# Two unused margins in SBUF: other start addresses for the operands of a two-block kernel

## The reference

```
h   = modulate(rms_norm(x, g), shift, scale)            # first block
p   = h @ w_in                                          # 2048 x 3904
x   = x + gate * (rms_norm(concat(att, conv)) @ w_out)  # 2048 x 2048
u   = dwconv3(hf @ w_up)                                # 2048 x 11008
x   = x + gate * ((a * silu(g)) @ w_down)               # 5504 x 2048
z   = rms_norm(x) @ w_in_2                              # second block, 2048 x 10248
m   = sigmoid(g_a) * (A @ w_proj_a) + sigmoid(g_b) * (B @ w_proj_b)
x   = x + m @ w_out_2
x   = x + square(relu(rms_norm(x) @ w_up_2)) @ w_down_2 # 2048 x 8192 x 2048
out = rms_norm(x)
```

## Time and profile before

| | |
|---|---|
| median of 3 runs | 2872.16 us (2868.47 to 2873.35) |
| profiled execution, its own time | 2872.42 us |
| its span | 2870.6 us |
| TensorE busy | 2684.6 us (94%), weight loads 2571.9 us (90%) |
| VectorE, ScalarE busy | 1794.6 us (63%), 1224.7 us (43%) |
| granted TensorE clock, mean | 0.959 |
| DMA | 552.93 MB, mean 193 GB/s |

### The profile page before, as it was taken

One profiled execution on the slowest core, in us unless ns is written; L12 is line 12 of the kernel. 1 busy time (PEld: TensorE's weight loads), 2 busy tenths in 40 slices (PEclk: granted clock), 3 DMA queues, 4 the chain that ended last, 5 costly groups with the idle time before them and its releaser, 6 DMA issues.

```text
span 2870.6 us, 52211 instructions
## 1 busy us (share of the span) xinstructions
PE 2684.6 (94%) x21408; PEld 2571.9 (90%) x21408; DVE 1794.6 (63%) x2056; ACT 1224.7 (43%) x1407; POOL 20.8 (1%) x24
## 2 busy tenths in 40 slices
PE   4959977768899999999999999999999999999998
PEld 3659975348899999999999999999999999999998
DVE  3988965678766776576556455555555555555554
ACT  2733331223455554354454344444444443434433
POOL 0000000000000000000000000000000000000000
PEclk9989987769999999999999899999999999999999
DMA  4958953427566656656556455566556666666562
GB/s 156 384 195 315 331 171 120 147 88 282 188 191 201 195 182 204 192 163 220 183 171 186 130 173 166 161 188 199 196 178 184 191 197 192 190 196 193 196 206 103
DMA packets 288834, 552.93 MB, mean 193 GB/s; under 512 B 19434, under 2 KB 28632, under 8 KB 288024
## 3 DMA queue, kind: packets, MB, share of 16 engines
q1 hardware_dynamic: 287416, 548.10, 59.2%
q10 hardware_dynamic: 1248, 2.42, 0.3%
HBM read 548.35 MB, written 2.10 MB: 192 GB/s over the span
## 4 chain that ended last, share of the span: by engine, by line
PE 86%; DVE 9%; issue 2%; ACT 2%; DMA 1%; ACTq 1%; DVEq 0%; SPq 0%
PE half L1627 25%; PE half L1629 25%; PE half L1628 25%; DVE wlo L909 2%; PE half L1683 1%; DVE acc L931 1%; PE half L1661 1%; PE half L1663 1%; DVE acc L928 1%; PE half L1662 1%; DVE tmp L1233 1%; DMA raw<-in_w_ada 1%; PE half L1832 1%; PE half L1821 1%; PE half L1822 1%
## 5 line engine op out<-in xcount | busy, mean ns | idle before, releaser
L909 DVE TENSOR_TENSOR wlo<-raw,whi 128x1024 fp32r<-128x1024 f32 (+2 forms) x917 | 1096.7, 1209 | 815.8 <-ACT whi L511 813.6
L511 ACT ACTIVATE whi<-raw 128x1024 fp32r<-128x1024 f32 (+2 forms) x917 | 952.5, 1048 | 1195.0 <-PE half L1629 1033.6
L1627 PE MATMUL half<-hf,whi 128*128 128x256 f32 x2400 | 663.9, 277 | 6.2 <-DVE hf L986 5.1
L1628 PE MATMUL half<-hf,whi 128*128 128x256 f32 x2400 | 663.4, 276 | 0.0
L1629 PE MATMUL half<-hf,wlo 128*128 128x256 f32 x2400 | 663.4, 276 | 0.0
L1627 PE MATMUL half<-hid,whi 128*128 128x256 f32 x1712 | 474.0, 277 | 0.0
L1628 PE MATMUL half<-hid,whi 128*128 128x256 f32 x1712 | 473.4, 276 | 0.0
L1629 PE MATMUL half<-hid,wlo 128*128 128x256 f32 x1712 | 473.4, 276 | 0.0
L1627 PEld LDWEIGHTS half<-hf,whi 128*128 128x128 f32 x2400 | 451.4, 188 | 7.0 <-issue 5.5
L1629 PEld LDWEIGHTS half<-hf,wlo 128*128 128x128 f32 x2400 | 451.3, 188 | 0.0
L1628 PEld LDWEIGHTS half<-hf,whi 128*128 128x128 f32 x2400 | 451.2, 188 | 0.0
(11 more groups left out here) (253 smaller groups left out, 3092.0 us busy)
## 6 DMA issues: line engine op xcount, KB each, us to landing
raw<-in_w_up SPq DMA_DIRECT2D x288, 512.0 KB, 4.4
raw<-in_w_in SPq DMA_DIRECT2D x216, 512.0 KB, 4.1
raw<-in_w_down SPq DMA_DIRECT2D x212, 512.0 KB, 4.1
raw<-in_w_ada SPq DMA_DIRECT2D x192, 512.0 KB, 5.7
raw<-in_w_out SPq DMA_DIRECT2D x64, 512.0 KB, 4.7
raw<-in_w_proj_a SPq DMA_DIRECT2D x16, 512.0 KB, 3.7
raw<-in_w_proj_b SPq DMA_DIRECT2D x16, 512.0 KB, 4.2
raw<-in_w_up SPq DMA_DIRECT2D x16, 384.0 KB, 3.5
```

Source lines behind the costliest of these rows:

```text
L511: A(whi[:, s, 0:elems], raw[:, c, 0:elems], ACT.Copy).then_inc(s_hi_ready, 1)
L909: V.tensor_tensor(wlo[:, s, 0:elems], raw[:, c, 0:elems], whi[:, s, 0:elems].bitcast(F32), ALU.subtract).then_inc(s_drained, 1)
L1627: mm(o, hi, x[:, 0:T], start=(k == 0 and b % 2 == 0), stop=False, skip_group_check=True)
L1628: mm(o, hi, x[:, T:2 * T], start=False, stop=False, skip_group_check=True)
```

## The change

Two buffers are allocated that nothing reads or writes: 224 float32 (896 bytes) in each partition below `xt`, and 144 float32 (576 bytes) below the first scope. All instructions and their order stay.

```
@@ -239,6 +239,7 @@
         score_bank, turn_bank, head_bank, sum_bank = [halves[i // 2][:, 2 + i % 2, :] for i in range(4)]
 
 
+        sb("lower_margin", [P, 224])
         xt = sb("xt", [P, KT, T])
         raw = sb("raw", [P, NRAW, CW])
         whi = sb("whi", [P, NSPLIT, CW], F32R)
@@ -265,6 +266,8 @@
         rtok = sb("rtok", [P, 4])
         square_sum = sb("square_sum", [P, TB, 4])
 
+
+        sb("upper_margin", [P, 144])
 
         first = ExitStack()
         t16 = sb("t16", [P, KT, T], scope=first)
```

## The result

The changed kernel takes 2980.69 us (median of 4 runs, 2974.29 to 2982.92), the kernel before 2872.76 in the runs beside it (2868.47 to 2873.70): a ratio to it of 1.0375, 95% interval 1.0356 to 1.0394. It is slower by 108 us, where 13 us less was forecast, and outside the range. The profiled execution took 2981.47 us, with a span of 2979.7 us and a mean granted clock of 0.960 (0.959 before).

A forecast was written before the change was run, and what follows sets the result against it. TensorE was taken as the bound, by matmul count times start-to-start distance. Slow-rhythm matmuls speeding up (-12 us) and 512-column products (-1) made -13 us on 2872.42, giving 2859 us; range 2785 to 2910, the forecast's own 2854 to 2866.

The forecast's parts named there:

- Reading of the bound: Weight products, lines 1627 to 1629: time is mostly number of matmuls times start-to-start distance; TensorE busy 94% of the span.
- Fast stretches: Nearly everything after 761 us, 13,700 weight-product matmuls 113.3 ns apart: no change, zero, bounds -59 and +64 us.
- Its upper bound: Those 13,700 matmuls after 761 us would at worst start 118 ns apart, +64 us.
- Slow stretches: 26 stretches of weight products, 360.5 us at 118 ns a matmul: would fall to 113.3 ns, -12 us.
- The slow rhythm spreads: Rival, 27%: weight-product matmuls after 761 us go from 113.3 to 118 ns; 2904 us with half, 2936 with all.
- The fast rhythm gets faster: Rival, 12%: weight-product matmuls drop from 113.3 to 109 ns, a transpose's distance; -77 us, 2795 us.
- The rule against it: TensorE's moving operand and weights have independent read ports, so reads don't meet, no placement matters, and the sum is zero.
- Token products: Lines 1661 to 1663, 384 matmuls of 512 columns: from 229 to 226.7 ns each, -1 us.
- DMA: `raw` moves to a 256-byte multiple; three `w_ada` waits of about 8 us, 97 to 136 us: counted as zero.
- Vector and scalar engine: Same instructions at other addresses, any few ns on a 1.2 us split hidden by four slots: zero.

The follow-up runs named there:

- The lower margin alone: Kernel before with only the 896 bytes below `xt` added (weights 0, moving operands 704 modulo 1024): 2875.71 us, ratio 1.0011.
- the fast version: Kernel before with weights and moving operands both starting 16 bytes into longer tiles, no added margin: 2860.95 us, ratio 0.9955; with `raw` on a multiple of 256 too, 2861.28 us.
- the two fast versions: Kernel before with moving operands 16 bytes into longer tiles behind 160 bytes: 2861.78 us; or with weights and moving operands both 16 bytes in, no margin: 2860.95 us.

## Why the prediction was wrong, step by step

- **Reading of the bound: right.** TensorE's distance from start to start sets the time, and it depends on addresses. The step "whether that distance depends on addresses" was the right question. The counts in it held too: 13,700 of line 1627 to 1629 in the long stretches, 3,060 slow ones (3,150 counted).
- **Fast stretches: this step failed, and it is the one that cost the forecast.** "I take zero: it is the row with the most residues in it, and none of them moved it." The residues in that row all had the same distance. Blocks of 512 bytes, steps of 2048 and 4096, and the `qn` product's 256 are multiples of 256, and `qn` and the other moving operands (64 and 832) differ by a multiple of 256 from one another. The row varied everything but the one quantity that counts, and the change set that one from 192 to 0. In place of zero the term was 13,700 x 6.67 = +91 us for the matmuls that it counted, and +106 us with the shorter stretches that it left out.
- **Its upper bound failed too.** 118 ns was taken as the slowest because it was the slowest row of the kernel before. The runs have 120.0 at distance 0 and 123.3 at distance 4; the term itself, 91 us, lies outside the bound of 64 that was set for it. A bound from rows holds for the placements in the rows.
- **Slow stretches: wrong in sign.** "The change makes each weight block lie within one 512-byte multiple" was offered as what ends the collision, -12 us. The slow stretches went to 120.0 ns as well, +7 us. That weight load and moving read meet fits what the runs show, since the time follows the difference of their two addresses and changes with the size of the load; the step of the meeting itself is not shown. That staying within 512 bytes avoids it is refuted. The lower margin alone does exactly this, at a ratio of 1.0011. The 14 us were to be had, by starts 16 bytes off a multiple of 32: the ratios of 0.9927 and 0.9955.
- **The rivals and their chances.** "The slow rhythm spreads" had the place (the long stretches) and the direction right, and nearly the reason (the distance becomes a multiple of 128; 128 itself costs 5.3 to 6.7 ns, 0 costs 6.7). It had a price of 4.7 ns where 6.7 was due, and its sign, records of 281 ns, did not come in either: they are 283. It was given 27%, and the forecast 32%, on an argument about block boundaries for which no row spoke, while the table of addresses had the distance going from 64 to 0 modulo 128. "The fast rhythm gets faster" is refuted for this change, and no placement tried in any run has a stream of 256-column matmuls under 113.3, loads of a quarter of the size included.
- **The rule against it: wrong as a reason, here.** The changed kernel's 283 and 192 ns rows, and the streams with nothing but TensorE at work, show placement costing up to 6.7 ns on 113.3, and 10 in a stream at distance 4. The Trainium skill (TensorE: Matmul & The Clock Gate, Step-by-step) has two independent read ports, by which no placement would matter; the measurement decides against drawing that from it.
- **Token products: right**, 229.0 to 227.1 ns, -0.7 us against -1.
- **DMA: zero was right for the sum, though the rate did move.** `raw` on a multiple of 256 raises the rate by 20 in 387 GB/s. The three 8 us waits for `w_ada` of the earlier trace rows have left the chain, whose shares from 80 to 180 us are now as below; 24.1% of the same window was `w_ada` before, with 28.3% of issue and 19.2% of splits. The loads no longer pace this stretch, but splits and issue are next in line. No gain is seen: the products begin at 170.5 to 173.1 us in the four kernels with `raw` at 0 and at 171.9 to 174.3 in the eight others, and the fast version's time is the same with it and without. The Trainium skill (DMA: Bandwidth & Descriptors, How a descriptor splits into AXI transactions) starts every transaction of a read on a 256-byte multiple; an estimate by that rule is 68 beats against 64 for 2 KB, 6%. The packets of 2 KB in this window took 88.6 against 84.0 ns, 5%: near it in size, though what is off the multiple here is where the packets are written.

```profile
by line: issue 41.5%; DVE wlo L912 30.8%; PE half L1721 7.2%; DVE row L1038 3.8%; PE half L1630 3.5%; PE half L1631 3.0%; PE half L1632 3.0%; DVE acc L934 3.0%; DVE acc L931 2.3%; DVEq L963 0.7%; DVE mod_a L963 0.7%; DVEq L118 0.4%; DVE acc
```

- **Vector and scalar engine: right.** A split has a median of 1225 ns after and 1224 before.

What stays open. No run shows why steps of 16 bytes have such an irregular effect, nor why a weight address off a multiple of 32 spoils distance 112 and helps distance 192. I found no rule for the phase in which a stream begins, and by the two groups of run times not even the same kernel always begins alike. No run took the load away altogether: that the surcharge needs the load is concluded from its dependence on both addresses and from the shorter loads, one size of which made it more frequent at distance 112.

## What to carry to other kernels

Where TensorE is the bound and each matmul has its own weight load, compare the start of the moving operand minus that of the weights, modulo 256 bytes, before and after any change of allocation: a buffer that nobody uses cost 3.6% here, and 64 bytes more gave the changed kernel over a third of its loss back. Aligning both operands to the same multiple of 256 made the slowest whole programs here, so time the candidates in a small stream first with the shapes and the sides of the real one, since at 512 columns the order of the distances is another. And before a row is used as evidence that "addresses don't matter", write down the one quantity the change moves, and look whether that row varies it.

## What the hardware showed that I had not expected

- A 256-column matmul with a 128-column load beside it starts every 113.3 to 123.4 ns at the upper clock (113.3, 117.8 and 120.0 above all), by the distance of its operands modulo 256, whether they start on a multiple of 32, and the phase. 113.3 is 17/16 of 106.7, which is 256 columns at 2.4 GHz; at 1.2 GHz the distance is 213.3, 256 columns without anything on top, and placement did not show.
- With 128 moving columns a 128-column load leaves no gain from the shorter matmul and no effect of the distance: 111.7 ns at 0, 64 and 112 alike, with loads of 192 ns. That the load is the limit there is likely; no run made it shorter.
- A stream keeps a rhythm for thousands of matmuls once it is in it. The same program on the same chip took 2868 or 2895 us, most likely by it, and the 13 runs of the two fast versions lie within 5 us.
- An SBUF start off a multiple of 256 costs incoming 2 KB packets 5% (387 against 407 GB/s, at 128 and 192 past the multiple).
